# Late expert slots of the first kind: the order of the products of 384 and of 192 columns

## What is computed

```python
def block(xb):                                   # h2, the tokens after the second norm
    q = jnp.einsum('td,de->te', xb, w_q)...      # queries, scores against two sets of 128 keys
    ...                                          # top 16 of 256 pairs -> eidx (128 experts a token), gw
    u = exp_u[eidx]
    v = exp_v[eidx]
    a = jax.nn.gelu(jnp.einsum('td,thkd->thk', xb, u).astype(jnp.float32))
    return jnp.einsum('thk,thkd->td', (gw * a).astype(dt), v)
```

## Time and profile before

| | |
|---|---|
| median of 3 runs | 1907.99 us (1907.52 to 1908.73) |
| profiled execution | 1907.44 us |
| its span, first to last instruction | 1905.7 us |
| TensorE busy | 1870.9 us (98%) |
| VectorE busy | 1436.6 us (75%) |
| ScalarE busy | 840.9 us (44%) |
| GpSimd busy | 345.1 us (18%) |
| mean granted TensorE clock | 0.994 |

### The profile page before, as it was taken

One profiled execution on the slowest core, in us unless ns is written; L12 is line 12 of the kernel. 1 busy time (PEld: TensorE's weight loads), 2 busy tenths in 40 slices (PEclk: granted clock), 3 DMA queues, 4 the chain that ended last, 5 costly groups with the idle time before them and its releaser, 6 DMA issues.

```text
span 1905.7 us, 27526 instructions
## 1 busy us (share of the span) xinstructions
PE 1870.9 (98%) x11300; PEld 1685.0 (88%) x11300; DVE 1436.6 (75%) x1863; ACT 840.9 (44%) x1138; POOL 345.1 (18%) x216
## 2 busy tenths in 40 slices
PE   7999999999989999999999999999999999999997
PEld 7998999889889999999777889889899898898895
DVE  5434555567663598896888898988988989989886
ACT  4334555444443101223555455455455454454552
POOL 1000123000000001101333223322222323223200
PEclk9999999999989999999999999999999999999999
DMA  8545433745343766889899989999999999999881
GB/s 312 199 177 202 152 133 111 308 177 221 133 156 123 269 256 250 342 330 340 338 359 370 372 343 367 386 351 381 377 349 393 361 353 396 360 356 390 349 317 48
DMA packets 100206, 548.34 MB, mean 288 GB/s; under 512 B 8704, under 2 KB 33344, under 8 KB 35952
## 3 DMA queue, kind: packets, MB, share of 16 engines
q1 hardware_dynamic: 53424, 374.37, 51.7%
q0 software_dynamic: 20096, 147.04, 18.9%
q10 hardware_dynamic: 26560, 25.17, 4.3%
HBM read 530.74 MB, written 14.68 MB: 286 GB/s over the span
## 4 chain that ended last, share of the span: by engine, by line
PE 96%; DVE 1%; DMA 1%; ACT 1%; issue 1%; SPq 0%; POOL 0%; DVEq 0%; ACTq 0%
PE bank L565 16%; PE bank L925 14%; PE bank L827 11%; PE bank L580 9%; PE bank L927 7%; PE bank L858 6%; PE bank L861 6%; PE bank L859 6%; PE bank L857 6%; PE bank L860 6%; PE bank L847 2%; PE bank L793 1%; DMA ring_raw<-in_stream 1%; PE bank L605 1%; PE bank L660 1%
## 5 line engine op out<-in xcount | busy, mean ns | idle before, releaser
L1317 DVE TENSOR_TENSOR ring_lo<-ring_raw,ring_hi 128x2048 fp32r<-128x2048 f32 (+1 forms) x94 | 206.5, 2200 | 207.0 <-ACT ring_hi L989 206.8
L1763 DVE TENSOR_TENSOR split_a<-experts,split_a 128x2048 fp32r<-128x2048 f32 x120 | 274.6, 2288 | 53.4 <-ACT split_a L1242 53.1
L1242 ACT CAST split_a<-experts 128x2048 fp32r<-128x2048 f32 x120 | 229.6, 1914 | 141.0 <-PE bank L861 140.0
L925 PE MATMUL bank<-h_split,split_a 128*128 128x384 f32 x944 | 270.8, 359 | 0.0
L565 PE MATMUL bank<-actT_hi,ring_hi 128*128 128x256 f32 x896 | 259.2, 289 | 11.0 <-DVE ring_lo L1322 8.2
L565 PE MATMUL bank<-actT_lo,ring_hi 128*128 128x256 f32 x896 | 254.4, 284 | 0.0
L565 PE MATMUL bank<-actT_hi,ring_lo 128*128 128x256 f32 x896 | 254.4, 284 | 0.0
L927 PE MATMUL bank<-h_split,split_a 128*128 128x192 f32 x944 | 236.3, 250 | 0.0
L533 POOL DMA_INDIRECT rows<-in_peer_u,eidx x64 | 139.7, 2183 | 449.0 <-DVE rows L1670 443.7
L533 POOL DMA_INDIRECT rows<-in_peer_v,eidx x64 | 152.9, 2389 | 368.5 <-DVE hrow L1676 344.9
L827 PE MATMUL bank<-h2T,experts 128*128 128x192 f32 x1280 | 216.3, 326 | 0.0
(11 more groups left out here) (278 smaller groups left out, 3764.0 us busy)
## 6 DMA issues: line engine op xcount, KB each, us to landing
experts<-in_stream SPq DMA_DIRECT2D x221, 1024.0 KB, 7.4
ring_raw<-in_stream SPq DMA_DIRECT2D x95, 1024.0 KB, 4.8
late_raw<-in_stream SPq DMA_DIRECT2D x35, 1024.0 KB, 7.5
gate_matrix<-stage ACTq DMA_DIRECT2D x12, 1024.0 KB, 4.9
gbuf<-gate_matrix ACTq DMA_DIRECT2D x16, 768.0 KB, 13.0
gb<-in_ln_g POOLq DMA_DIRECT2D x3, 1024.0 KB, 4.8
gb<-in_ln_b POOLq DMA_DIRECT2D x3, 1024.0 KB, 9.6
act_raw<-in_xT SPq DMA_DIRECT2D x4, 512.0 KB, 7.8
```

Source lines behind the costliest of these rows:

```text
L925: pe.matmul(b[:, 0:2 * ND], hi[:, w], h2_split[:, ko].rearrange("p c t -> p (c t)"), start=(ko == 0), stop=False, skip_group_check=True)
L1242: act.copy(split(m)[0], tile).then_inc(split_hi, 1)
L1317: dve.tensor_tensor(ring_lo[:, r, 0:n], ring_raw[:, r, 0:n], ring_hi[:, r, 0:n].bitcast(F32), ALU.subtract).then_inc(lo_ready, 1)
L1763: dve.tensor_tensor(lo, raw_slot(split_slot(m))[0], hi.bitcast(F32), ALU.subtract).then_inc(split_lo, 1)
```

## The change

In a slot of the first kind the tiles are taken in twos. First come the long products of both tiles, then the short products of both. Weights, columns, output columns and the number of products stay. `start` still stands on the long product of tile 0 and `stop` and the increment on the short product of tile 15, which is still the slot's last.

```diff
-                        for ko in range(KO):
-                            w = slice(ko * P, (ko + 1) * P)
-                            pe.matmul(b[:, 0:2 * ND], hi[:, w], h2_split[:, ko].rearrange("p c t -> p (c t)"), start=(ko == 0),
-                                      stop=False, skip_group_check=True)
-                            last = pe.matmul(b[:, 0:ND], lo[:, w], h2_split[:, ko, 0, :], start=False, stop=(ko == KO - 1),
-                                             skip_group_check=True)
+                        for k2 in range(0, KO, 2):
+                            for ko in (k2, k2 + 1):
+                                pe.matmul(b[:, 0:2 * ND], hi[:, ko * P:(ko + 1) * P], h2_split[:, ko].rearrange("p c t -> p (c t)"),
+                                          start=(ko == 0), stop=False, skip_group_check=True)
+                            for ko in (k2, k2 + 1):
+                                last = pe.matmul(b[:, 0:ND], lo[:, ko * P:(ko + 1) * P], h2_split[:, ko, 0, :], start=False,
+                                                 stop=(ko == KO - 1), skip_group_check=True)
```

## The result

The changed kernel takes 1911.27 us (median of 12 runs), the kernel before, run beside it, 1907.60 (12 runs): a ratio of 1.0022 over all the runs, with a 95% interval of 1.0014 to 1.0030. The medians are 3.7 us apart, the means 4.1. The kernel has become slower, where the prediction had -1.4 us. 1911.27 us lies inside the predicted range, but a ratio of 1 lies outside the interval, so this is a slowdown and not "the same".

A forecast was written before the change was run, and what follows sets the result against it. TensorE's own pace of products was taken as the bound. Terms of -3 and +1 ns gave -2 ns a quad, over 704 quads -1.4 us, from 1907.99 to 1906.6 us; range 1902.0 to 1912.5 us.

The forecast's parts named there:

- The second long product: In each quad, no longer behind a short product: 173.3 ns against 176, -3 ns, bounds 170 and 179.
- the loads: In each quad, two weight loads show before and after, 15 ns each; pairing moves them and removes none.
- rivals A and B: First: loss sits in size changes, 1895.3 us, chance 0.08. Second: loads run further ahead, 1882.7 us, chance 0.03.
- the Trainium skill's reorder window: TensorE's queue pulls weight loads ahead; the forecast took one load ahead, against several loads ahead at 1882.7 us.
- the recorded starts of 0.20, 0.17, 0.09 and 0.11 us: Sign expected in TensorE's timeline of a changed quad, in place of 0.20, 0.09, 0.20, 0.09.
- the first long and the first short product keep their neighbour ahead: 0: In each quad, these two products keep their cost: 0, with 1 or 2 ns to both sides.
- The second short product: In each quad, now behind a short product: 109 ns against 108, +1 ns, bounds 107 and 112.
- all of this costs nothing: Around the slots: same products, loads and waits, same last product and increment, distances to slot's end kept; no cost.
- Rival C: Handovers between like products in a quad cost more: +14 ns a quad, +9.9 us, 1917.9 us, chance 0.07.

The follow-up runs named there:

- x16: The kernel before, with all sixteen long products of a slot first, then all sixteen short ones: 1910.60 us, ratio 1.0015.
- s256_pair: The changed kernel's order, with short products of 256 columns in place of 192: 1922.29 us (one run).
- x4: The kernel before, with four long products, then four short ones, in place of alternating: 1914.26 us, ratio 1.0040.

## Why the prediction was wrong

What bounds the kernel was read rightly: no wait came in, and the whole loss is TensorE's own pace. Three points held. The second long product fell from 176 to 174 ns (173.3 said). Nothing was gained on the loads: two show in a quad before and after, so rivals A and B are out, and with them the reading of the Trainium skill's reorder window ("TensorE: Matmul & The Clock Gate", "Architectural detail: the array is 16× 32×32, not 1× 128×128") as several loads ahead; the loads of the changed kernel still start one product ahead, within 0.03 us of the record of the product before. And the recorded starts of 0.20, 0.17, 0.09 and 0.11 us came as written, so this sign of being right did not tell the forecast from what happened.

Two steps failed.

The step "the first long and the first short product keep their neighbour ahead: 0". The first long product went from 176 to 180 ns, +4, the only one of the four terms that left its bounds (1 or 2 ns to both sides). The second short product went to 111, +3 where I took +1, within its bounds; less the 2 ns of the second long one that is +4.4 ns a quad, 704 x 4.4 = +3.1 us where I had -1.4. The mistake under it was to take the steps between load starts as each product's own price, fixed by what stands just ahead. x16 shows that a product pays for others: there an uncovered load costs 111.7 ns, and the long products behind the short ones pay 17.5 ns more than their own. In the kernel before, 108.3 stood on the short product and 2.8 on the long one behind it, 111.1 together, near that price. So it is likely that the 3 ns that I let vanish were part of the load's price, and came up elsewhere. The row that had this price, 112 ns for an uncovered load, I set aside as another format. With it the quad would be 2 x (173.3 + 112) = 570.6 ns, 1.7 over the measured 568.9, +1.2 us: nearer, and still 2.7 ns short of the 573.3. But that sum is the same for both orders, so it does not forecast the loss either. That pairs lose where a load shows, and how much, is measured here (4.4 ns with two loads that show in a quad, 6.7 with one); what in TensorE makes them lose stays open.

The step "all of this costs nothing", for what stands behind the slots. The last product is the same and no wait moved, but the value products have two paces, and the changed kernel enters them always at the slower one: +1.1 us. The rows of before held the hint: one group of value products took 36.72 us and the next 36.92, from the same instructions. I read one group alone, and of its five products only that some steps were longer.

That the time lies inside the range is partly luck: the range was made wide for the steps of the products, of which one still left its bounds, and +1.1 us come from a stage that had no room in it at all.

Rival C had the sign, and more than the size (+9.9 us), but for another reason: like products side by side cost nothing in ten groups of eleven when no load shows (s256_pair).

## What to carry to other kernels

Where a product is shorter than the load behind it, try to spread these products out: at the sizes here alternating with long ones was the cheapest of the orders tried, and pairing them cost 4.4 to 6.7 ns in four products. Price a moved product by the length of the whole repeated pattern, as the trace or a trial shows it, and not by the single steps in it. And before a stage is called untouched, compare its repeats in the profile of before: if the same instructions take two times, what is put ahead of them can choose between the two.

## What the hardware showed that I had not expected

The lengths of repeated patterns are whole or half multiples of 13.33 ns: 120.0 (9) for 256 columns, 226.7 (17) for 512, 853.3 (64) for three alternating pairs, 573.3 (43) for the quad, 1153.3 (86.5) for x4, 4573.3 (343) for x16, 586.7 (44) and 580.0 (43.5) for the quads with 256 columns, 1146.7 (86) and 1153.3 (86.5) for five value products, and 1180.0 (88.5) for the two quads that repeat in the first group of s256_pair. The two new costs fit in as such steps: 42.67 became 43, and 86 became 86.5. Why they settle there, no run shows: all column counts here are multiples of 32, and 32 columns at 2.4 GHz, the clock of this stage (granted 1.00 in the earlier trace rows), are 13.33 ns, so it may be that and fixed overheads alone. I did not expect either that it is so exact: in every kernel each group's length repeats to 1 ns once its pattern is reached, over 730 us and with the DMA share at 0.9, so a difference of 0.04 us in a group can be read from one profile where the kernel's time needs many runs to show 2 us.
